# The even layer's block outputs with blocks as rows, its decay rows spread with 128 rows of weights, and four smaller edits

## Time and profile before

| | |
|---|---|
| median of 3 runs | 2978.79 us (2972.84 to 2979.21) |
| the profiled execution | 2975.73 us, of which 2973.9 us are the span in the trace |
| PE busy | 2810.5 us, 95% of the span |
| DVE, ACT, POOL busy | 1459.1 us, 949.5 us, 202.2 us |
| mean granted TensorE clock | 0.971 of full speed |
| DRAM traffic | 93 GB/s over the span |

### The profile page before, as it was taken

One profiled execution on the slowest core, in us unless ns is written; L12 is line 12 of the kernel. 1 busy time (PEld: TensorE's weight loads), 2 busy tenths in 40 slices (PEclk: granted clock), 3 DMA queues, 4 the chain that ended last, 5 costly groups with the idle time before them and its releaser, 6 DMA issues. The chain is left out here.

```text
span 2973.9 us, 34050 instructions
## 1 busy us (share of the span) xinstructions
PE 2810.5 (95%) x12640; PEld 2245.9 (76%) x12640; DVE 1459.1 (49%) x1894; ACT 949.5 (32%) x1287; POOL 202.2 (7%) x209
## 2 busy tenths in 40 slices
PE   6999999969999999999988999999999999699997
PEld 5788777547888878888766788887777677488885
DVE  5566347655444344443475544423887335433323
ACT  4432223233333233322234333222224442333212
POOL 3000114101000000000210000000000000000000
PEclk9999999779999999999999999999999999799998
DMA  3344325223333222332311233333441133133321
GB/s 120 113 124 135 126 97 161 62 85 93 99 99 104 94 83 94 99 106 92 110 50 43 92 99 96 114 104 110 135 124 44 43 99 99 47 95 99 106 96 38
DMA packets 82457, 284.69 MB, mean 96 GB/s; under 512 B 14753, under 2 KB 15393, under 8 KB 81473
## 3 DMA queue, kind: packets, MB, share of 16 engines
q1 hardware_dynamic: 71424, 250.54, 26.7%
q0 software_dynamic: 6336, 26.70, 2.8%
q10 hardware_dynamic: 4608, 6.30, 0.9%
HBM read 262.26 MB, written 14.94 MB: 93 GB/s over the span
## 5 line engine op out<-in xcount | busy, mean ns | idle before, releaser
L177 DVE TENSOR_TENSOR wl<-raw,wh 128x1024 fp32r<-128x1024 f32 (+2 forms) x440 | 574.2, 1306 | 1062.7 <-ACT wh L171 1051.8
L223 PE MATMUL PS<-Hh,wl 128*128 128x512 f32 x2232 | 879.7, 394 | 44.2 <-DVE wl L177 20.5
L224 PE MATMUL PS<-Hh,wh 128*128 128x512 f32 x2232 | 872.5, 391 | 0.0
L225 PE MATMUL PS<-Hl,wh 128*128 128x512 f32 x2232 | 872.4, 391 | 0.0
L171 ACT ACTIVATE wh<-raw 128x1024 fp32r<-128x1024 f32 (+2 forms) x440 | 480.1, 1091 | 1145.3 <-PE PS L225 975.5
L223 PEld LDWEIGHTS PS<-Hh,wl 128*128 128x128 f32 x2232 | 421.3, 189 | 148.8 <-issue 51.7
L225 PEld LDWEIGHTS PS<-Hl,wh 128*128 128x128 f32 x2232 | 421.1, 189 | 88.8
L224 PEld LDWEIGHTS PS<-Hh,wh 128*128 128x128 f32 x2232 | 421.5, 189 | 87.8 <-issue 1.5
L225 PE MATMUL PS<-ffn_gl,wh 128*128 128x512 f32 x880 | 350.5, 398 | 0.0
L223 PE MATMUL PS<-ffn_gh,wl 128*128 128x512 f32 x880 | 346.1, 393 | 2.8 <-DVE wl L177 2.8
L224 PE MATMUL PS<-ffn_gh,wh 128*128 128x512 f32 x880 | 348.2, 396 | 0.0
(11 more groups left out here) (409 smaller groups left out, 2599.1 us busy)
## 6 DMA issues: line engine op xcount, KB each, us to landing
raw<-in_gu SPq DMA_DIRECT2D x220, 512.0 KB, 3.6
raw<-in_dn SPq DMA_DIRECT2D x80, 704.0 KB, 4.1
raw<-in_hin SPq DMA_DIRECT2D x44, 512.0 KB, 4.3
raw<-in_oin SPq DMA_DIRECT2D x16, 512.0 KB, 3.7
raw<-in_hin_gate SPq DMA_DIRECT2D x16, 512.0 KB, 3.6
X<-QKV ACTq DMA_DIRECT2D x96, 64.0 KB, 3.2
kept_x<-X POOLq DMA_DIRECT2D x16, 256.0 KB, 3.6
raw<-in_eout SPq DMA_DIRECT2D x8, 512.0 KB, 3.7
```

Source lines behind the costliest of these rows:

```text
L177: self.nc.vector.tensor_sub(self.wl[j % SPLIT][:, 0:kw], self.raw[j][:, 0:kw], self.wh[j % SPLIT][:, 0:kw].bitcast(F32)).then_inc(self.lo_ ...
L223: self.nc.tensor.matmul(out, wl, xh[:, u.k0 + k, :], start=first, stop=False)
L224: self.nc.tensor.matmul(out, wh, xh[:, u.k0 + k, :], start=False, stop=False)
L225: done = self.nc.tensor.matmul(out, wh, xl[:, u.k0 + k, :], start=False, stop=last)
```

## The change

1. `outputs(q)`: the operands change places. The blocks are the weights (128 rows by 64 columns) and the tables the moving data (128 columns); two groups go to the two halves of the partitions of PSUM, as in `heads`. The table `KT` is kept group by group, so its slice for a group is contiguous. `outputs(q-1)` now stands ahead of `heads(q-1)` in PE's loop and waits for `add_input(q-2)` (`added`) where it waited for the eviction.
2. `turn_outputs(q)`, new, after `heads(q)`: sixteen float32 products of a 64x64 piece with an identity, which bring the evicted outputs back to channels on the partitions, in PSUM. The 36 small transfers through DRAM are gone. `add_input(q)` reads PSUM and moves one quarter earlier in DVE's loop; `add_input(3)` and all four GELUs are in this stage.
3. `spread_a(h)`: the weights are column h of the 128x128 identity, repeated 128 times, and `AT` has 128 rows, 120 of which GpSimd has set to zero.
4. The squares of the heads' outputs move from the next stage into this one (three of four), and in the next stage PE sums the squares ahead of unit 0, with four tiles rounded after the one square that is left.
5. `hybrid_input`: the swap of tile n is issued by ACT one unit later, ahead of its wait for the next unit's result, and no longer stands between a copy and the next `split_hi`. For tiles from 8 on, `rotate` writes its last sum with the tokens grouped by residue.
6. `window_attend`: L2081 then reads 128 contiguous elements.

```diff
@@ -837,6 +837,7 @@
         g.memset(self.co.ones8[:], 1.0).then_inc(self.filled, 1)
+        g.memset(self.AT, 0.0).then_inc(self.filled, 1)
@@ -855,8 +856,8 @@
         self.step(dve, v.tensor_scalar(x, self.DT[:], self.W[:, 6, 0:1], -1.0, ALU.mult, ALU.mult))
-        dve.wait_ge(self.filled, 1)
-        self.step(dve, v.tensor_tensor_scan(self.AT[:], self.co.ones8[:], x, 0.0, ALU.mult, ALU.add))
+        dve.wait_ge(self.filled, 2)
+        self.step(dve, v.tensor_tensor_scan(self.AT[0:SSD_H, :], self.co.ones8[:], x, 0.0, ALU.mult, ALU.add))
@@ -1173,8 +1174,7 @@
             if k == 7:
-                a.activation(self.KT.rearrange("p (i g) -> p g i", g=S5G),
-                             self.co.PS[:, 7, :].rearrange("p (g i) -> p g i", i=16), ACT.Copy).then_inc(self.k_evicted, 1)
+                a.activation(self.KT, self.co.PS[:, 7, :], ACT.Copy).then_inc(self.k_evicted, 1)
@@ -1384,14 +1385,6 @@
             sp.dma_start(OUT.rearrange("p g n -> p (g n)"), d["s5_out"]).then_inc(arrived, 16)
-            for q in range(4):
-                sp.wait_ge(evicted, q + 1)
-                for l in range(BL):
-                    to = d["s5_y"].rearrange("(g i) l b -> l i g b", i=16)[l, :, 8 * q:8 * q + 8, :]
-                    sp.dma_start(to, Y8(q)[16 * l:16 * l + 16, :].rearrange("p (g b) -> p g b", b=NB)).then_inc(stored, 16)
-                if q < 3:
-                    sp.wait_ge(stored, 16 * BL * (q + 1))
-                    sp.dma_start(YL[:, q], d["s5_y"][q * P:(q + 1) * P]).then_inc(restored, 16)
@@ -1422,17 +1415,30 @@
                 if q >= 1:
-                    pe.wait_ge(evicted, q)
-                for g in range(8 * q, 8 * q + 8):
-                    out = co.PS[:, 3, NB * (g % 8):NB * (g % 8) + NB]
-                    mm(out, TOE[:, :, g::S5G].rearrange("p l i -> p (l i)"), U8[:, g, :], start=True, stop=False)
-                    m = mm(out, OUT[:, g, :], SB[:, q % 2, g % 8, 0:NB], start=False, stop=True)
+                    pe.wait_ge(added, q)
+                for j in range(4):
+                    out = lambda s: co.PS[NB * s:NB * s + NB, 3, j * P:(j + 1) * P]
+                    for s in range(2):
+                        g = 8 * q + 4 * s + j
+                        mm(out(s), U8[:, g, :], TOE[:, :, 16 * g:16 * g + 16], start=True, stop=False)
+                    for s in range(2):
+                        g = 8 * q + 4 * s + j
+                        m = mm(out(s), SB[:, q % 2, g % 8, 0:NB], OUT[:, g, :], start=False, stop=True)
                 m.then_inc(out_done, 1)
...
+            def turn_outputs(q):
+                pe.wait_ge(evicted, q + 1)
+                for l in range(BL):
+                    for s in range(2):
+                        p = NB * s
+                        m = mm(co.PS[p:p + NB, 3, NB * l:NB * l + NB], YB(q)[p:p + NB, NB * l:NB * l + NB],
+                               co.ident[p:p + NB, p:p + NB], start=True, stop=True)
+                m.then_inc(out_turned, 1)
...
                     pe.wait_ge(seg_ready, h - 1)
-                mm(co.PS[:, 4 + h % 2, :], co.ident[0:SSD_H, h:h + 1].broadcast_to([SSD_H, P]), AT[:], start=True,
+                mm(co.PS[:, 4 + h % 2, :], co.ident[:, h:h + 1].broadcast_to([P, P]), AT[:], start=True,
@@ -1451,11 +1457,13 @@
                 if q >= 1:
+                    outputs(q - 1)
                     heads(q - 1)
-                    outputs(q - 1)
+                    turn_outputs(q - 1)
...
             heads(3)
+            turn_outputs(3)
@@ -1475,7 +1483,14 @@
                 act.wait_ge(out_done, q + 1)
-                nc.scalar.activation(Y8(q), co.PS[:, 3, :], ACT.Copy).then_inc(evicted, 1)
+                nc.scalar.activation(YB(q).rearrange("p (l j i) -> p j l i", l=BL, i=16),
+                                     co.PS[:, 3, :].rearrange("p (j l i) -> p j l i", l=BL, i=16),
+                                     ACT.Copy).then_inc(evicted, 1)
...
+            def square(c):
+                act.wait_ge(gated, c + 1)
+                act.wait_ge(out_done, c + 1)
+                nc.scalar.activation(SQ[:, c, :], XC[:, c, :], ACT.Square).then_inc(squared, 1)
@@ -1490,8 +1505,11 @@
                 power(2 * q + 1)
+                if q >= 2:
+                    square(q - 2)
             evict(3)
-            for c in range(3):
+            square(2)
+            for c in range(4):
@@ -1553,9 +1571,12 @@
             def add_input(q):
-                dve.wait_ge(restored, 16 * (q + 1))
+                dve.wait_ge(out_turned, q + 1)
                 dve.wait_ge(gated, q + 1)
-                through(co, v, U, YL, Z, q, cols).then_inc(added, 1)
+                k = cols["s5_d"] + q
+                v.scalar_tensor_tensor(Z[:, q, :].rearrange("p (b l) -> p l b", l=BL), U[:, q], co.cols[:, k:k + 1],
+                                       co.PS[:, 3, :].rearrange("p (l b) -> p l b", b=NB), ALU.mult,
+                                       ALU.add).then_inc(added, 1)
@@ -1565,21 +1586,13 @@
                     skip(q - 1)
-                if q >= 2:
-                    add_input(q - 2)
-            add_input(2)
+                    add_input(q - 1)
             skip(3)
...
-def through(co, v, U, YL, YB, c, cols):
...
-    k = cols["s5_d"] + c
-    return v.scalar_tensor_tensor(YB[:, c, :].rearrange("p (b l) -> p l b", l=BL), U[:, c], co.cols[:, k:k + 1],
-                                  YL[:, c], ALU.mult, ALU.add)
+            add_input(3)
 @stage
-def finish_halves(co, st, Y, YB, U, YL, T, SQ, M, cols, stored):
+def finish_halves(co, st, Y, YB, T, SQ, M, cols):
@@ -1611,14 +1620,11 @@
         def _(pe):
-            def sums(n):
-                if n == 0:
-                    for c in range(4):
-                        pe.wait_ge(squared, c + 1)
-                        m = nc.tensor.matmul(co.PS[:, 4 + c // 2, :], co.ones[:], SQ[:, c, :], start=c % 2 == 0,
-                                             stop=c % 2 == 1)
-                    m.then_inc(summed, 1)
-            co.multiply(pe, st, bank_free, chunk_ready=g_parted, between=sums)
+            pe.wait_ge(squared, 1)
+            for c in range(4):
+                m = nc.tensor.matmul(co.PS[:, 4 + c // 2, :], co.ones[:], SQ[:, c, :], start=c % 2 == 0, stop=c % 2 == 1)
+            m.then_inc(summed, 1)
+            co.multiply(pe, st, bank_free, chunk_ready=g_parted)
@@ -1626,14 +1632,9 @@
                 nc.scalar.activation(G[0][:, c, :], T[:, c, :], ACT.Copy).then_inc(g_rounded, 1)
-            for c in range(3):
+            nc.scalar.activation(SQ[:, 3, :], Y[:, 3, :], ACT.Square).then_inc(squared, 1)
+            for c in range(4):
                 round_g(c)
-            for c in range(4):
-                nc.scalar.activation(SQ[:, c, :], Y[:, c, :], ACT.Square).then_inc(squared, 1)
-            act.wait_ge(skipped, 1)
-            nc.scalar.activation(T[:, 3, :], YB[:, 3, :], ACT.Gelu_apprx_tanh).then_inc(gelued, 1)
-            act.wait_ge(gelued, 1)
-            round_g(3)
@@ -2078,8 +2075,8 @@
                         p = HD * s
-                        m = mm(co.PS[:, 2 * (k % 2) + s, (1 + g) * P:(2 + g) * P], QKV[p:p + HD, 8 * g + c, r::4],
-                               QKV[p:p + HD, 8 * g + 4 + c, r::4], start=True, stop=True)
+                        m = mm(co.PS[:, 2 * (k % 2) + s, (1 + g) * P:(2 + g) * P], QKV[p:p + HD, 8 * g + c, r * P:(r + 1) * P],
+                               QKV[p:p + HD, 8 * g + 4 + c, r * P:(r + 1) * P], start=True, stop=True)
@@ -2281,6 +2278,14 @@
+            def swap(n):
+                c = n % RAW
+                if n >= RAW:
+                    act.wait_ge(done, n - RAW + 1)
+                for q in range(4):
+                    p, o = 32 * q, 32 * (q ^ 1)
+                    act.dma_start(B[p:p + 32, c], QKV[o:o + 32, n:n + 1, :]).then_inc(swapped[c], 16)
@@ -2291,15 +2296,14 @@
                         act.wait_ge(gated, RAW)
+                    else:
+                        swap(n - 1)
...
                     act.sem_inc(bank_free, 1)
-                    if i > first_qk:
-                        act.wait_ge(done, RAW * (i - first_qk - 1) + c + 1)
-                    for q in range(4):
-                        p, o = 32 * q, 32 * (q ^ 1)
-                        act.dma_start(B[p:p + 32, c], QKV[o:o + 32, n:n + 1, :]).then_inc(swapped[c], 16)
+                elif i == first_v and c == 0:
+                    swap(RAW * (first_v - first_qk) - 1)
@@ -2317,7 +2321,9 @@
                 dve.wait_ge(cosines, n + 1)
-                nc.vector.tensor_add(one(QKV, n), A[c % 2], B[:, c]).then_inc(done, 1)
+                to = one(QKV, n) if n < 8 else QKV[:, n, :].rearrange("p (r q) -> p q r", r=4)
+                by = (lambda t: t) if n < 8 else (lambda t: t.rearrange("p o (q r) -> p (o q) r", r=4))
+                nc.vector.tensor_add(to, by(A[c % 2]), by(B[:, c])).then_inc(done, 1)
```

(24 more changed lines are left out.)

17 lines of the change are left out of this document (7 added, 10 removed).

## The result

The changed kernel takes 2943.11 us (median of 4 runs, 2941.23 to 2948.38) beside 2977.53 for the kernel before on the same chip (4 runs). The ratio is 0.989, with a 95% interval from 0.9872 to 0.9907: 34 us or 1.1% faster. The forecast was 2957, its range 2946 to 2973: the direction is right, and the gain is larger than the range allowed. The profiled execution took 2943.38 us.

A forecast was written before the change was run, and what follows sets the result against it. PE was taken as the bound, busy 95% of the span and at low clock in the even mixer. Terms -12.4 - 6 - 2.7 = -21.1 us took 2975.73 to 2954.6; with 3.06 for the median, 2957.7, rounded to 2957; range 2946 to 2973.

The forecast's parts named there:

- One sign: Even mixer's middle stage: granted clock near 1.00 from its first turn on, listed among what would show the forecast.
- The loop: Even mixer's middle stage: DVE sets the period at 14.42 us against PE's 12.7; its turns end at 594.1.
- The tail: Middle stage after the loop: outputs 5.0, heads 4.5, turning 2.4 us; next stage starts at 608.2, a gain of 8.2.
- The better rival: Whole kernel: clock kept through tail and sums, 5 us more, hybrid stage reaches its 9: 2949 us; chance 0.06.
- The first rival: Even mixer's spreads: zero rows do not count, clock stays as before; 2981.5 us, no change; chance 0.13.
- no drain shows: PE's tiling modes: 8-row product to 128-row one takes 2.01 us, within its own 2.07, so no draining cost seen.
- Hybrid input: Hybrid mixer's input stage: moving swap issues off split_hi's path gains 6 us; bounds +7 to -9.
- little of the slower units: Hybrid input: small gain added to the 5.6 us of PE idle time, making 6.
- What I feared for the rotation: Hybrid input: late swap makes DVE wait, next split_lo stands behind; about 0.7 us left by the schedule.
- The rival with DVE behind: Hybrid input: swap lands too late or regrouped writes fill DVE's slack; 2963 to 2970 us; chance 0.09.
- Window attention: Window attention stage: contiguous reads save 0.3 us per step, half comes through: 2.7 us gained; bounds 0 to -4.8.
- none is on PE's path: Hidden work (36 transfers, three squares on ACT, memset of AT, copy of KT): claimed not to hold PE.

The follow-up runs named there:

- the swap in place: Changed kernel with the hybrid input's four swap transfers issued behind each copy, as before the change: 2953.57 us, ratio 0.9937 to the kernel before.
- the normalisation cut in two: Changed kernel with the next stage's second normalisation half behind low parts of units 2 and 3, rounding behind the sigmoids: 2938.34 us, ratio 0.9862 to the kernel before.

## Why the prediction was right and wrong

Most of the mechanism was right: the clock rises in the first turn, DVE sets the period, PE waits for `add_input` ahead of the outputs in the third and fourth turn and in the tail, the swap no longer holds `split_hi`. One sign did not come: I had the clock near 1.00 from the first turn on, and it reads 0.88, 1.00 and 0.89 in the next three, with falls behind waits. It cost little, for DVE's `add_input` stayed 14.41 us apart in spite of it. The sum was short of the gain by 13.9 us (2957 to 2943.1). In the profiled executions the gain is 32.35 us against 21.1, 11.25 more; the remaining 2.6 are that the forecast's median stood 3.06 above its profiled execution and the new one 0.27 below, less 0.7 of rounding. The 11.25 are 4.7 up to the sums, 3.2 in the hybrid input, 4.4 in all the rest, less 1.1 in window attention.

- **The loop: right.** Its end was forecast at 594.1. It came at 595.83 (594.70 + 1.13), and the stage began 1.78 us later than before (536.27 against 534.49), so 594.1 to within 0.1.
- **The tail: the step that failed in the middle stage.** Outputs(3), heads(3) and the turning were priced at 5.0, 4.5 and 2.4, and took 3.28, 2.26 and 1.08. That is 5.3 less, of which 0.7 went to the rest of the tail. Two errors add up. The heads were taken at the low clock and ran at the high one, since the clock came back at the end of the outputs: 2.2 us. The outputs were nearly all at the low clock, as forecast, and still 1.7 shorter, because the rate of L2104 was too dear: at the high clock the new ones take 1.82 us (554.63 to 556.45) where I had 2.65. The turning takes 1.08 in every turn where I had 1.7 at the high level, and no clock explains that part. The sums took 5.36 us where 5.5 was forecast. The better rival had a kept clock here, at 5 us: the size was near, by luck, since the clock was not kept through the outputs. Its hybrid stage at 9 us is what came. What lies between its 2949 and the 2943 is in stages that no case had.
- **The stage's own spread.** The changed kernel's 75.1 us is the lowest of five executions with this code, whose mean is 76.9. Of the 4.7 us, some 1.8 may be no more than that.
- **The first rival: wrong in its reason, and its price too.** The spreads over 128 rows do raise the clock. And with the rows taken away the kernel is not at 2981.5 but at 2948.2. I had read the earlier trace rows for where the clock rises and not for where it falls: between the pair of 0.65 us at 559.92 and `swap_states` with 2.02 at 565.83 stand the old outputs alone. The rival priced the middle stage as longer than before with 8 rows; it is 5.6 us shorter, and the next stage gives 4.2 more, as forecast.
- **The added rows are not free, they are a gain.** I took 2.01 us from an 8-row product to a 128-row one for an undisturbed step. Between products of 128 rows the step is 1.81, so "no drain shows" was misread: each step between an 8-row product and a 128-row one took 0.1 to 0.2 us longer than between two of 128 rows.
- **Hybrid input: right in kind, 3.2 too small.** The 5.6 us of idle time went, as forecast. The "little of the slower units" is not 0.4: an instruction of PE took 139.39 / 601 = 0.232 us in the earlier trace rows and takes 145.00 / 641 = 0.226 now, 3.7 us over 641 of them. What I feared for the rotation did not come: the swap lands in 2.0 us (3.2 before), and DVE waits 1.0 us in all for it. The regrouped sum costs 0.41 us more (0.69 to 1.10), near the 0.45 that I had. The rival with DVE behind is refuted, though the swap in place shows its 2.2 us.
- **Window attention: right only by two errors that cancel.** L2078 takes 0.71 us per step, not 1.0, so PE saves 0.59 in each of 16, or 9.4 us. Of this 4.4 to 4.8 come through at equal clock: ACT's chain holds about half, as I had said. In the changed kernel the stage's lower clock took most of that again, and 1.6 are left where 2.7 was forecast.
- **Unedited stages: not in the forecast at all.** Busy times of two stages that the change does not touch, the chunk attention and the stretch behind the gates, first in the kernel before, then in the changed one:

```profile
1541.91:1603.37 61.46, 52.55 (x393) 36.42 (x393) 33.74 (x140) 36.03 (x105) 0.00 (x0) 0.92 0.00 1
2442.27:2578.08 135.81, 104.88 (x403) 77.39 (x403) 74.28 (x91) 40.27 (x58) 10.82 (x9) 0.88 0.26 85
```

```profile
1526.34:1585.63 59.29, 49.46 (x393) 34.25 (x393) 33.84 (x140) 35.99 (x105) 0.00 (x0) 0.97 0.00 1
2413.26:2547.34 134.08, 103.19 (x403) 76.84 (x403) 74.27 (x91) 40.25 (x58) 10.79 (x9) 0.90 0.27 86
```

The same instructions, 2.2 and 1.7 us shorter, at a higher clock (0.97 against 0.92, 0.90 against 0.88). With the normalisation cut in two they were back at 61.45 and 136.28. The changed kernel on another chip gave 59.97 and 134.21, within 0.7 and 0.1 us. So between kernels the low stretches fall elsewhere in stages that no edit touches, and that was worth some 2 us for each of these two, in either direction. The rest of the 4.4 is 1.6 us less behind the second of them, 0.7 in between, and 1.8 more ahead of the middle stage. That last part I had put at nothing ("none is on PE's path"): the middle stage begins at 534.2 and 534.5 us in the two kernels without the change and at 535.3 to 536.9 in the ten executions with it or with most of it. Why is not shown. The range reached 11 us below the forecast, to the better case with window attention at its bound, and left no room for this beside it.

## What to carry to other kernels

In a timeline at a low clock, look for two places, where it rises and where it falls, and name what PE did before each: here it rose out of spreads over 128 rows, worth some 5 to 7 us, and fell in the old outputs, which I had not looked at. Before a gain between two landmarks is put down to one edit, cut it at the stage boundary: of the 9.8 us that the other edits gave, 4.2 came from the order of two jobs in the next stage. A group's mean can mix shapes: 963 ns for the last sum of the rotation was four of 693 and eight of 1100. Where a stage ends with an engine that has idled, price the products behind the wait at the low level only until the trace shows such a row returning. And queue what nobody waits for (a swap's issue, the second half of a normalisation) behind the weight split that PE waits for: that was 9 to 11 us and 6 us here.

## What was unexpected of the hardware

- A product over 32 or 64 rows left the clock where 8 rows did (stage 81.1 and 82.2 us against 82.5), and only the one over 128 rows let it rise in the first turn (75.1 to 78.8), with zeros or with ones in the added rows. The 32 and 64 rows and the ones were run once each.
- The clock fell while PE was at work without a gap, in products of 128x128 weights with 64 moving columns (0.39 to 0.63 us for a pair). With the operands exchanged it fell too, behind waits of 1.4 us and more.
- From a spread over 8 or 64 rows to the 128-row product behind it it is 2.00 us at the low clock; between products of 128 rows 1.81.
- A weight load that reads with a step of four took 322 ns against 195, and its product, whose moving data have the same step, 457 against 308, means over the stage.
- The stage of window attention, its code unedited between them, took from 66.7 to 70.5 us in eight kernels, longer where its clock was lower, and repeated to 0.02 us for the same kernel on another chip; the middle stage of that kernel did not (75.1 and 76.4).
